# Two row tiles per round in the delta-net stage: inversions of eight heads, four chunks of the recurrence beside them

## The reference, cut to what matters

```
a_mat = where(strict, (k*beta) @ k.T * decay, 0)        # 64 x 64
sol   = triangular_solve(a_mat + eye, [v*beta, k*beta*exp(gc)])
qk    = (q @ k.T) * decay
def step(s, ...):                                        # one chunk after another
    v_new = u_i - w_i @ s
    o_i   = qd_i @ s + qk_i @ v_new
    s     = s * gl_i + kd_i.T @ v_new
```

## Time and profile before

| | us |
|---|---|
| median of 3 runs | 1504.05 (1503.1 to 1508.19) |
| span of the profiled execution | 1503.7 |
| `delta_net` stage, PE's first to last matmul | 302.96 to 908.14 |
| PE busy over the span | 1418.9 (94%) |
| DVE, ACT, POOL busy | 790.0, 636.8, 376.0 |

### The profile page before, as it was taken

One profiled execution on the slowest core, in us unless ns is written; L12 is line 12 of the kernel. 1 busy time (PEld: TensorE's weight loads), 2 busy tenths in 40 slices (PEclk: granted clock), 3 DMA queues, 4 the chain that ended last, 5 costly groups with the idle time before them and its releaser, 6 DMA issues. The chain is left out here.

```text
span 1503.7 us, 32493 instructions
## 1 busy us (share of the span) xinstructions
PE 1418.9 (94%) x13360; PEld 1189.7 (79%) x13360; DVE 790.0 (53%) x1504; ACT 636.8 (42%) x1441; POOL 376.0 (25%) x366
## 2 busy tenths in 40 slices
PE   6999999879999999999999997998998999799996
PEld 5999998868888888888888884664665766687785
DVE  5665666413334333334533325885888886545442
ACT  4454555411112212112211115884665666655551
POOL 0022223222122132222332103550002000055553
PEclk9999999989999999999999998998999999999998
DMA  8644526394443245432145616134100003566651
GB/s 242 183 130 142 157 88 173 110 204 124 130 134 97 70 115 145 129 95 72 51 121 162 178 47 184 61 115 121 44 15 1 15 28 94 159 175 189 202 168 63
DMA packets 203334, 177.93 MB, mean 118 GB/s; under 512 B 30131, under 2 KB 188984, under 8 KB 203192
## 3 DMA queue, kind: packets, MB, share of 16 engines
q1 hardware_dynamic: 154489, 118.42, 27.0%
q0 software_dynamic: 28256, 46.35, 11.0%
q10 hardware_dynamic: 20446, 11.14, 3.0%
HBM read 107.79 MB, written 65.59 MB: 115 GB/s over the span
## 5 line engine op out<-in xcount | busy, mean ns | idle before, releaser
L817 PE MATMUL acc<-side_rows,side_w 128*128 128x384 f32 (+2 forms) x2448 | 458.0, 335 | 15.8 <-ACT side_stage L836 7.8
L817 PEld LDWEIGHTS acc<-side_rows,side_w 128*128 128x128 f32 x2448 | 393.4, 191 | 33.2 <-ACT side_stage L836 7.9
L2047 DVE TENSOR_TENSOR_SCAN prod<-keepb,prod 128x512 f32<-128x512 f32 (+4 forms) x184 | 203.3, 1146 | 52.4 <-ACT keepb L1973 44.5
L709 PE MATMUL acc<-side_rows,side_w 128*128 128x384 f32 (+1 forms) x864 | 149.3, 330 | 0.0
L1282 DVE COPY base<-b_two 128x256 f32<-128x256 f32 x85 | 36.1, 424 | 214.0 <-PE b_two L1071 214.0
L709 PEld LDWEIGHTS acc<-side_rows,side_w 128*128 128x128 f32 x864 | 142.4, 188 | 1.9
L836 ACT ACTIVATE side_stage<-acc 128x384 f32<-128x384 f32 (+2 forms) x102 | 46.8, 461 | 210.9 <-PE acc L817 188.7
L2172 PE MATMUL b_y<-whi,mhi 128*128 128x512 f32 x272 | 108.0, 397 | 8.8 <-DVE wlo L2256 7.6
L1991 ACT ACTIVATE wt<-b_w 128x512 f32<-128x512 f32 (+5 forms) x188 | 88.1, 522 | 58.6 <-PE b_w L1905 58.4
L2172 PE MATMUL b_y<-wlo,mhi 128*128 128x512 f32 x272 | 106.6, 392 | 0.0
L2172 PE MATMUL b_y<-whi,mlo 128*128 128x512 f32 x272 | 106.4, 391 | 0.0
(11 more groups left out here) (249 smaller groups left out, 2314.3 us busy)
## 6 DMA issues: line engine op xcount, KB each, us to landing
side_rows<-hs_scratch POOLq DMA_DIRECT2D x16, 1536.0 KB, 10.3
hs_scratch<-side_rows SPq DMA_DIRECT2D x34, 512.0 KB, 4.7
side_rows<-hs_scratch POOLq DMA_DIRECT2D x6, 1344.0 KB, 10.7
base<-in_x_prompt SPq DMA_DIRECT2D x15, 512.0 KB
mixed<-mix_scratch SPq DMA_DIRECT2D x15, 512.0 KB, 6.7
gates<-sz_scratch SPq DMA_DIRECT2D x15, 512.0 KB, 8.0
xres<-in_x_prompt SPq DMA_DIRECT2D x15, 512.0 KB
out_y_prompt<-yy POOLq DMA_DIRECT2D x15, 512.0 KB, 6.6
```

The costliest lines, as they stand in the source:

```text
L709: last = pe.matmul(acc[:, u % 2, 0:w], side.w[:, c, w_, k, :], h_[:, b % 2, k, 0:w], start=(k == 0 and p == 0), stop=(k == KT - 1 and p == 2))
L817: last = pe.matmul(self.acc[:, n % 2, 0:width], w[:, w_part, k, :], rows[:, row_part, k, 0:width], start=(k == 0 and i == 0), stop=(k == K ...
L2047: dve.tensor_tensor_scan(prod[0:R, hh, c0:c0 + nk][:, ::-1], kv, kv, prod[0:R, hh, c0 + nk:c0 + nk + 1], ALU.mult, ALU.bypass).then_inc(pr ...
```

## The change

A round now prepares a pair of tiles (8 heads; the ninth pair has one tile) and runs the four chunks of the pair before: 9 rounds and a last one with only the recurrence, where there were 17 and one. `turn_x` is 4 transposes, `level_y` and `level_x` are 16 products each, the copies by ACT and DVE 512 columns wide. The side pieces are dealt out anew, 80 in a round of two tiles. `outputs` is called once for a tile and issues its products alternately for chunk 0 and chunk 1. POOL makes the masked matrices 512 wide. The state's part of an output (`state_part`) is taken as soon as it is there. DVE's `split_low` stands at points of its own. `previous_rows` loads two tiles in each round. The first round needs two tiles of q, k and v.

```diff
-                POINTS = [8, 5] + [4, 1] * 5 + [4]
+                SLOTS = [6, 12, 8, 6, 4, 7, 4, 7, 4, 7, 4, 7, 4]
+                TAIL = [4] * 6 + [8] + [0] * 6
+                POINTS = [SLOTS] * NP + [TAIL]
...
                         def kq(g):
+                            pe.wait_ge(tile_in, 32 * tiles_to(g + 1))
...
-                        def outputs(c):
-                            m, half = c // 2, part(c % 2)
-                            pe.wait_ge(vn_kept, c + 1)
+                        def outputs(m):
+
+                            pe.wait_ge(vn_kept, 2 * m + 2)
                             for h in range(4):
-                                last = pe.matmul(b_vn[half, 1, h], qk[half, m % 2, h], vn[half, h], start=True, stop=True)
+                                for half in (part(0), part(1)):
+                                    last = pe.matmul(b_vn[half, 1, h], qk[half, m % 4, h], vn[half, h], start=True, stop=True)
...
-                            invert(1, [lambda: new_values(c)], [lambda: update_state(c)])
-                            invert(2, [lambda: read_state(c + 1), lambda: outputs(c)], [lambda: new_values(c + 1)])
-                            invert(3, [lambda: update_state(c + 1)], [lambda: outputs(c + 1)])
-                            invert(4)
-                            invert(5)
+                            beside(g, 1)
+                            if new:
+                                rows(2 * g)
                             if old:
-                                outputs_transposed(m - 1)
+                                new_values(c)
+                            beside(g, 2)
+                            if new and len(pairs[g]) == 2:
+                                rows(2 * g + 1)
+                            if old:
+                                update_state(c)
+                                if g >= 2:
+                                    outputs_transposed(2 * g - 3)
...
+                            beside(g, 3)
+                            if new:
+                                turn_x(g, 1)
+                                level_y(g, 1)
+                            if old:
+                                read_state(c + 1)
+                            beside(g, 4)
+                            if new:
+                                level_x(g, 1)
+                            if old:
+                                new_values(c + 1)
...
# on ACT
-                                if m == 0:
-                                    previous_rows()
+                            keep_beside(g, (1,))
+                            if new:
+                                keep_values(2 * g)
+                            if after:
+                                load_tile(after[0])
+                            keep_beside(g, (2,))
+                            if new and len(pairs[g]) == 2:
+                                keep_values(2 * g + 1)
+                            if g >= 2:
+                                keep_outputs(2 * g - 3)
+                            if new:
+                                previous_rows(g)
+                                keep_turned(g, 1)
...
# on DVE
-                            split_beside(m, (0, 1, 2) if l == 1 else (2 * l,))
...
+                            if old:
+                                values(c)
+                            if new:
+                                first_inverse(g)
+                            split_beside(g, (1,))
+                            if two:
+                                keep_keys(2 * g + 1)
+                            if old:
+                                new_state(c)
+                            split_beside(g, (2,))
+                            if new:
+                                keep_y(g, 1)
```

More of the change, by code:

```diff
@@ L1039, in rows @@
                             last.then_inc(rows_ready, 1)
[L1041 to L1048, removed]
-                                        last = pe.matmul(b_kq[part(c), b, a], qk_ring[part(b), m % 3, 2 + a, tok], qk_ring[part(b), m % 3, a:a + 3:2, tok],
-                                                         start=True, stop=True)
-                            last.then_inc(kq_ready, 1)
@@ new lines, in beside @@
+                        def beside(g, point):
+                            side.products(pe, FIRST[g][point], POINTS[g][point])
+                        for g in range(NP + 1):
+                            new, old = g < NP, g > 0
+                            c = 4 * (g - 1)
+                            second = old and c + 2 < 2 * TILES
+                            beside(g, 0)
+                            if new:
+                                decay(g)
+                                kq(g)
@@ new lines, in _ @@
+                            if new:
+                                turn_x(g, 2)
+                                level_y(g, 2)
+                            if old:
+                                update_state(c + 1)
+                                outputs(2 * g - 2)
+                            beside(g, 6)
+                            if new:
+                                level_x(g, 2)
+                            if second:
+                                read_state(c + 2)
+                            beside(g, 7)
@@ new lines, in _ @@
+                            if new:
+                                turn_x(g, 3)
+                                level_y(g, 3)
+                            if second:
+                                new_values(c + 2)
+                            beside(g, 8)
+                            if new:
+                                level_x(g, 3)
+                            if second:
+                                update_state(c + 2)
+                            beside(g, 9)
+                            if new:
+                                turn_x(g, 4)
+                                level_y(g, 4)
@@ new lines, in _ @@
+                            if second:
+                                read_state(c + 3)
+                            beside(g, 10)
+                            if new:
+                                level_x(g, 4)
+                            if second:
+                                new_values(c + 3)
+                            beside(g, 11)
+                            if new:
+                                turn_x(g, 5)
+                                level_y(g, 5)
+                            if second:
+                                update_state(c + 3)
+                                outputs(2 * g - 1)
```

523 lines of the change are left out of this document (297 added, 226 removed).

## The result

| | before | after |
|---|---|---|
| median, us | 1503.57 (1502.87 to 1508.19) | 1463.78 (1461.88 to 1466.13, 4 runs) |
| span of the profiled execution | 1503.7 | 1464.3 |
| first matmul of the stage to the first of the next stage | 302.96 to 911.98 = 609.02 | 304.12 to 872.34 = 568.22 |
| from there to the end of the span | 591.7 | 592.0 |

The ratio is 0.9729, 95% interval 0.9716 to 0.9742. The spans differ by 39.4 us and the stage by 40.8; the forecast was 1462, 41.6 us less. What follows the stage takes the same time in both. One execution of the kernel with all three later edits took 1546.13 us at a mean granted clock of 0.84 and is left out of its numbers; all others ran at 0.97 to 0.98.

What follows compares the result with a forecast made beforehand. PE's queue was taken as the bound. Terms -29.6 - 3.6 - 2.4 - 9.1 - 6.4 + 3 + 6 + 0.5 sum to -41.6 us, from 1503.7 to 1462 us; range 1451 to 1476.

Steps and rivals of the forecast that it cites:

- levels: Levels of the eight full pairs: fixed parts on PE paid once a pair, 0.74 us saved at each of 40, -29.6 us.
- recurrence: Recurrence products on PE: a pair costs 6.5 us where two tiles cost 6.8, -3.6 us in all (0 to 6).
- round heads: Head of each pair's round: kq's sixteen products save 0.16 us and one run of side matmuls fewer 0.15, -2.4 us.
- first-round stall: First round: PE's 7.58 us wait while ACT issues previous_rows for 17 tiles goes, with 1.5 us of lower clock, -9.1 us.
- splits and `values`: Two rounds with the second group's weight splits: L829 now stands behind values, so PE's lost time there goes, -6.4 us.
- first `kq`: First round's kq: PE comes earlier and two tiles must have landed, +3 us (1.5 to 6).
- late weights, seventh round: turn_x of level 1, seventh round: fifth tile's raw weights land late, 4.3 us wait and 1.7 for the clock, +6 us.
- the end: End of the stage: POOL issues the four stores of the states behind the last outputs' products instead of ahead, +0.5 us.
- rival of groups bound by issue: Levels: each further eight products cost the full 0.39 us, so levels save 17.6 instead of 29.6; 1474 us, chance 0.13.
- Cover: Usual rounds: side matmuls cover level_x's wait for DVE's y copy (at most 0.85 us) and POOL's doubled masks; no other wait.
- rival of late row blocks: POOL's side-row loads, behind double-length masks, take 16 us or more; PE stops up to 5 us; 1480 us, chance 0.07.
- the slower one: level_x of 40 pair levels waits for DVE's or ACT's copy; a chain 2.5 us longer gives 1514 us; chance 0.04.

Runs made afterwards that it cites:

- all three later edits: Changed kernel with point 1's split_low early, 15 side pieces before the first round's kq, and ACT's root ahead of the last unit's copy: 1449.88 us.
- putting the cuts back: Changed kernel with three side matmuls moved into the middle of each level_y and level_x of the full pairs, 80 cuts: 1497.59 us.
- the kernel with that edit alone: Kernel before, with only previous_rows changed to load two tiles in each of the first nine rounds: 1505.05 us, ratio 1.0005.
- the kernel before with that edit: Kernel before, with only DVE's split_low moved from behind the copies of y to behind values, residual, new_state and finish: 1499.77 us, ratio 0.9963.

## Why the prediction was right, and where it was not

| term | predicted | the runs show |
|---|---|---|
| levels | -29.6 | 40 x (2.88 - 2.14) = -29.6; putting the cuts back costs 29 |
| recurrence, round heads | -3.6, -2.4 | a usual round -5.0, less 3.7 for levels: -1.3 x 8 = -10, about |
| first-round stall | -9.1 | -9.3 in the first round of the kernel with that edit alone, where later rounds give it back; the changed kernel has no wait for L836 |
| splits and `values` | -6.4 | -6.2 in the kernel before with that edit |
| first `kq` | +3 | +4.3 for the wait + 1.6 for the clock = +5.9 |
| late weights, seventh round | +6 | +6.4 |
| the end | +0.5 | +4.2 |
| sum | -41.6 | -38.6; stage measured -40.8 |

**Right by its mechanism.** The forecast rested on one reading: PE's queue is full, a group of small products has a fixed price each time it is set between side matmuls, and a pair pays it once. A level of a pair came out at 2.14 us, as worked out. The second eight products took 0.53 - 0.28 = 0.25 us (0.24 forecast), so the rival of groups bound by issue falls: 32 recorded instructions start in 0.53 us, 17 ns each. That is below the floor of about 25 ns in the Trainium skill, "TensorE: Matmul & The Clock Gate", section "Wait — 56ns, not 53.3ns?"; here the measurement decides.

**Right in size, incomplete in cause.** This is the stall's term. That the loads of two tiles could be taken "at the length of other issues and this wait at nothing" holds only where no unit ends just then. The run with that edit alone gave nothing, because ACT's issues then fell together with the ends of side units. What keeps them apart in the changed kernel, most likely its 80 pieces a round, was no part of my forecast: that this term came out is luck.

**Cover.** DVE's copy of y takes 0.69 us, under the bound of 0.85; but for the one forecast wait in the seventh round no level waited for DVE or ACT, and no round for its side rows, though their load took 11.9 us instead of 10.3. So neither the rival of late row blocks nor the slower one came.

**Mis-sized.** Three terms. *The first `kq`*: the wait grew by 4.3 us, and at 1.2 GHz its products took 1.92 us instead of 1.03 and the side matmuls behind them some 0.8 us more. I had given the second tile 1 to 4 us and nothing to the clock. *The recurrence and heads*: about 10 us instead of 6. By distances of starts in a usual round, two rounds of before against one of a pair, `update_state` and `outputs` together went from 3.38 to 2.31 us, `kq` from 1.18 to 0.93, the decays from 1.28 to 1.18, and `read_state` took 0.23 more. So the term that I had too small is that of `outputs` behind `update_state`. Alternating accounts for 0.2 of its 1.07 us (1.9 us in all); the rest I put down to one group of eight products in place of two of four, which no run tested. *The end*: I looked at POOL's stores and missed that ACT's root now stands behind the copy of the last side unit, which ends with the last side matmul. From there to the next stage it is 8.4 us and was 4.2 (907.76 to 911.98). These errors partly cancel (-4, +2.9, +3.7), so the total is closer than its parts deserve; about 2 us between the sum and the stage stay unexplained.

## What to carry to other kernels

Where one engine's queue is full, count its changes of shape and price one from start-to-start distances; joining two small groups is worth that price each time, even if no instruction goes. After a change of the loops, walk each other engine's order at the first round, the last and the one with unusual work: all three waits left here stood there, and three edits of a line or two took out 13.9 us. A stall removed at one place can come back in small waits at others (7.8 us in all, before and after), so time the edit by itself before crediting it.

## What the runs showed of the hardware

- Cutting one run of side matmuls by eight small products and back costs 0.37 us of PE's queue (80 cuts, 29 us), with no wait in the records.
- Runs of 32 recorded 64x64 instructions start every 17 ns, as those of 16 do.
- After a wait of 4.26 us PE ran at 1.2 GHz for some 4.5 us, which cost 2.1 us; after 5.43 us for some 3.6 us, which cost about 1.6. In the kernel with the levels cut, 1.2 GHz lasted some 15 us behind a wait of 4.37 us, and the round lost 4.6 us more than its cuts.
- The length of a wait alone does not tell what follows it: in the run with rows in pairs a wait of 2.20 us was once followed by full clock and once by a granted clock of 0.50, with 1.6 us lost over 21 side matmuls.
